# A gated-delta stage with paired transpositions, folded scales and another place for the norm sums

## Chip, cores, metric

One core of one Trainium2 chip runs the whole layer as one program. The metric is the device time of the program in microseconds; the median of three runs of the kernel before is 2038.25 (2031.85 to 2038.56).

## The reference, cut to what matters

One layer of a streaming encoder in float32: a norm, one input projection, chunk-band attention beside a gated delta branch, gates, an output projection and an MLP. The change lies in the gated delta branch (4 heads, key and value width 128, chunks of 64 tokens: 16 chunks of the prompt, and 128 sample tokens that this kernel treats as 2 more chunks). Per chunk and head:

```
k, q    L2-normalised over the 128 channels
gc      = cumsum(g);  decay[i,j] = exp(gc_i - gc_j) for i >= j
a_mat   = strict_lower(beta_i * (k_i . k_j) * decay[i,j]) + I
u, w    = solve(a_mat, [v * beta, k * beta * exp(gc)])
qk      = (q . k^T) * decay;  q_dec = q * exp(gc);  k_dec = k * exp(gc_last - gc)
v_new   = u - w @ s;  o = q_dec @ s + qk @ v_new
s       = s * exp(gc_last) + k_dec^T @ v_new       (chunk after chunk)
out     = rms_norm(o) * gain * silu(z)
```

## The kernel before, in words

The program runs in stages: norm, input projection, attention, delta, tail. The first two and the tail are long runs of products. `stage_delta` (from L1069) takes about 220 us of the span of 2028.7 us.

**Tiling.** 18 chunks of 64 tokens, in groups of four: groups 0 to 3 have four chunks, group 4 has two. Chunks 0 and 1 hold the sample streams, chunks 2 to 17 the prompt. The four heads are laid out as p = 0, 1 and x = 0, 1; x picks the lower or upper 64 partitions, so that one [128, 2, 64] tile holds a quantity of all four heads. Each float32 product appears as two records of the trace, a transposition as one. Chunk n of a group has its own PSUM bank B[n % 4] for its whole preparation.

**Preparation of a chunk**, in steps that go through the engines in turn:

- pair (PE L1702, DVE L1550, POOL L1361): PE multiplies k with q and k, DVE multiplies the result by the decay into KQ, POOL masks the part k.k^T into the levels M[0], M[1] of the block inverse.
- turn (PE L1709, ACT L1449, DVE L1562 and L1563, POOL L1378): PE brings k and v of the four heads from channels-by-tokens to tokens-by-channels, eight products with the identity; ACT writes U0 = v times the key's norm, DVE writes kbe = k exp(gc) and kd = k exp(gc_last - gc); POOL writes S0, a diagonal that holds the row scale s = beta / (norm squared of k).
- x0 (PE L1715, DVE L1570): PE multiplies M[0] by S0, DVE subtracts the result, scaled by s, from S0: the first inverse D, of blocks of two tokens, with the row scale carried in it.
- x0t (PE L1720, ACT L1454, POOL L1365 and L1371): D transposed; POOL makes the remaining levels of M and qk.
- levels 1 to 5, each in a half a (PE L1731, ACT L1466) and a half b (PE L1739, DVE L1582), double the block size of the inverse.
- solve, once for two chunks (PE L1749 and L1752, ACT L1464): w and u into WU.

**Scan.** Chunk after chunk: read (PE L1764 and L1768, ACT L1474, DVE L1592, POOL L1385), write (PE L1775, DVE L1596), out (PE L1780, DVE L1601, ACT L1486). The chunks of group g - 1 are scanned between the preparation steps of group g. For the sample chunks there are "heads" items instead: mask (POOL L1393, L1397), read, out, spread (DVE L1621) and write (PE L1811, DVE L1628), with POOL L1403 for the decay of the states.

**Once for a group.** decay (POOL L1344, PE L1676, ACT L1428); sums (POOL squares q and k in L1335, ACT does it for group 0 in L1433; PE L1682 sums over the channels; DVE L1534 copies the rows); cols (PE L1688 turns the rows into columns, ACT L1438 takes the square root, DVE L1538 to L1542 compute the reciprocal, s and -s); and for the group before, mean (DVE L1636, ACT L1496), norm (DVE L1640, L1641) and two turns (PE L1821, DVE L1649).

**Order.** `schedule()` writes one list by hand, with `between(g)` giving what follows each step of group g; every engine walks the list in its order and skips what it has no part in. So each engine's program order is fixed, and a wait holds up all that stands behind it on that engine. For group g and g + 1 the list reads: pair of the four chunks, then cols(g), then a scan read; turn of four chunks, a scan write; x0 of four, scan out and the next scan read; x0t of four, scan write; and so on; norm(g - 1) behind 4b, its turns behind 5a and 5b; solve, and behind it sums(g + 1).

**Loads.** SP loads the q, k, v channels of a group by `conv(g)` (L1283), one DMA of 12 x 128 rows with 256 tokens, 1 KB for each row (128 tokens, 512 B, for group 4), into C[g % 2]. conv(g) for g >= 2 is issued when the last scan read of group g - 2 is done (L1300), in the first half of group g - 1. Group 0 is loaded in the attention stage in two DMAs (L721 to L723), followed there by the loads of the attention's caches.

```
1116          if g == 1:
...
1118          if g:
1119              out["pair"].insert(0, ("grp", g, "cols"))
...
1124          if g + 1 < NG:
1125              out["2b"].append(("grp", g + 1, "decay"))
1126              out["solve"].append(("grp", g + 1, "sums"))
```

Of the kernel before, what the change touches and what calls it, by code (L numbers as in the profile page):

```python
# [570 lines left out]
def stage_attention(env):  # L571
# [22 lines left out]
    with ExitStack() as c:  # L594
# [90 lines left out]
        def _(sp):  # L685
# [42 lines left out]
            sp.wait_ge(env.c_in, 32)  # L728
# [340 lines left out]
def stage_delta(env):  # L1069
# [35 lines left out]
    def between(g):  # L1105
# [38 lines left out]
    def has(eng, item):  # L1144
# [3 lines left out]
        if kind == "prep":  # L1148
            return {"pair": ("pe", "dve", "pool"), "turn": ("pe", "act", "dve", "pool"), "x0": ("pe", "dve"),
# [46 lines left out]
    with ExitStack() as c:  # L1196
# [6 lines left out]
        C = [env.c0, at("c1", [P, CC, 4 * L], env.c_at + 4 * CC * 4 * L)]  # L1203
        top = env.c_at + 2 * 4 * CC * 4 * L
        o = [at(f"o{i}", [P, 4, 2, P], top + i * 4096) for i in range(2)]
        sq = [at(f"sq{i}", [P, HB, 4 * L], a) for i, a in enumerate((top + 2 * 4096, env.level_at))]
# [9 lines left out]
        S0 = [sb(f"s0{i}", [P, 2, L]) for i in range(4)]  # L1216
# [14 lines left out]
        eg, er, kn2, r2, s_, negs, nk, bq, ms, rso = (vec[:, i, :, :] for i in range(10))  # L1231
# [36 lines left out]

        def kind_of(n):
# [54 lines left out]
        def _(pool):  # L1324
            for item in SCHED:
# [3 lines left out]
                if kind == "grp" and s == "sums":  # L1329
                    w = L * len(GROUPS[n])  # L1330
                    pool.wait_ge(c_in[n % 2], 16 * ((n + 1) // 2))
                    wait(pool, "pe", "grp", n - 1, "sums")
                    for i in range(2):
                        half_c = C[n % 2][:, 4 * i:4 * i + 4, 0:w]
                        pool.tensor_tensor(sq[i][:, :, 0:w], half_c, half_c, ALU.mult).then_inc(sq_made, 1)  # L1335
# [1282 lines left out]
```

## Time and profile before

| what | value |
|---|---|
| median of three runs (lowest, highest) | 2038.25 us (2031.85, 2038.56) |
| the profiled execution: span | 2028.7 us |
| the profiled execution's own time | not listed; the page gives its span alone |
| mean granted clock of TensorE | 0.988 |
| PE busy over the span | 1945.0 us (96%) |
| delta stage, from its first product to the tail's first | 786 to about 1005 us |
| PE busy from 786 to 1006 us | 191.95 us |
| DVE, ACT, POOL busy from 786 to 1006 us | 119.63, 89.17, 96.47 us |

The span runs from the first to the last instruction; the lowest of the three runs is 3.15 us above it, the median 9.55 us. "x8" behind a row counts records: eight records of a product are the four heads of one chunk. Busy time of PE is the union of overlapping products, so a group's mean duration times its count is more than its busy time. What a row costs its engine is best read from the start of one row to the start of the next.

### The profile page before, as it was taken

Reading aid. Unit: us, or ns where it says so; the run is one execution under the profiler, and the core shown is the slowest. Engines: PE = TensorE matmul, PEld = TensorE weight load, DVE = VectorE, ACT = ScalarE, POOL = GpSimd, SP = SyncE. Lnnn points to the kernel's source line nnn. Section 1 sums busy time; section 2 is a strip of 40 time slices with the busy share of each in tenths; the row PEclk is TensorE's granted clock in tenths of the full one; section 3 lists DMA queues with packets and bytes.
Section 4 is the critical chain, followed back from the end, with each engine's and each line's share of the span. In section 5 each row is a group of like instructions: output and inputs, shape, how many; then the busy total and the mean of one; then the engine's idle time right before and its main releaser. Section 6 shows DMA issues by size and latency. Waiting matters only on the chain. (4 is left out here: it accounts for less than half of the span.)

```text
span 2028.7 us, 34282 instructions
## 1 busy us (share of the span) xinstructions
PE 1945.0 (96%) x14050; PEld 1759.9 (87%) x14050; DVE 746.8 (37%) x1482; ACT 634.4 (31%) x1283; POOL 590.6 (29%) x456
## 2 busy tenths in 40 slices
PE   7999999999998888899799999999999999999998
PEld 7899999999994566678699879999999999999997
DVE  5211777111125664565553182222222222222225
ACT  5101222100016664344443245222222222222222
POOL 3111111111132002543354144333333333333333
PEclk9999999999998998999899999999999999999999
DMA  4322223522227213131253232111111111111114
GB/s 119 108 89 88 76 88 118 209 88 88 88 97 238 92 64 84 44 96 39 62 158 105 104 125 88 47 43 42 42 42 42 42 42 42 42 42 42 42 60 169
DMA packets 159273, 169.22 MB, mean 83 GB/s; under 512 B 14187, under 2 KB 130043, under 8 KB 159150
## 3 DMA queue, kind: packets, MB, share of 16 engines
q1 hardware_dynamic: 152814, 141.52, 22.7%
q10 hardware_dynamic: 6336, 25.96, 3.2%
q8 instruction: 89, 1.46, 0.3%
q14 instruction: 34, 0.28, 0.0%
HBM read 126.84 MB, written 40.55 MB: 83 GB/s over the span
## 5 line engine op out<-in xcount | busy, mean ns | idle before, releaser
L2369 DVE TENSOR_TENSOR t_acc<-t_acc,t_B 128x512 f32<-128x512 f32 x252 | 173.3, 688 | 538.6 <-PE t_B L2475 538.6
L116 PE MATMUL i_ps<-x_hi,i_w_lo 128*128 128x384 f32 x1008 | 337.5, 335 | 0.0
L116 PE MATMUL i_ps<-x_hi,i_w_hi 128*128 128x384 f32 x1008 | 337.2, 335 | 0.0
L116 PE MATMUL i_ps<-x_lo,i_w_hi 128*128 128x384 f32 x1008 | 337.2, 335 | 0.0
L2462 PE MATMUL t_B<-t_merged_hi,t_wm_lo 128*128 128x384 f32 x768 | 256.9, 335 | 1.0 <-POOL t_wm_lo L2052 1.0
L2462 PE MATMUL t_B<-t_merged_lo,t_wm_hi 128*128 128x384 f32 x768 | 256.6, 334 | 0.0
L2462 PE MATMUL t_B<-t_merged_hi,t_wm_hi 128*128 128x384 f32 x768 | 256.6, 334 | 0.0
L106 POOL TENSOR_TENSOR i_w_lo<-i_w_raw,i_w_hi 128x1024 fp32r<-128x1024 f32 x44 | 105.4, 2395 | 433.4 <-ACT i_w_hi L101 433.4
L2052 POOL TENSOR_TENSOR t_wm_lo<-t_raw,t_wm_hi 128x1024 fp32r<-128x1024 f32 x49 | 118.8, 2425 | 295.9 <-ACT t_wm_hi L2127 295.9
L116 PEld LDWEIGHTS i_ps<-x_lo,i_w_hi 128*128 128x128 f32 x1008 | 189.8, 188 | 0.0
L116 PEld LDWEIGHTS i_ps<-x_hi,i_w_lo 128*128 128x128 f32 x1008 | 189.7, 188 | 0.0
L116 PEld LDWEIGHTS i_ps<-x_hi,i_w_hi 128*128 128x128 f32 x1008 | 189.6, 188 | 0.0
L2086 POOL TENSOR_TENSOR t_f_lo<-t_f,t_f_hi 128x384 fp32r<-128x384 f32 x96 | 97.5, 1016 | 212.6 <-ACT t_f_hi L2230 212.6
L101 ACT ACTIVATE i_w_hi<-i_w_raw 128x1024 fp32r<-128x1024 f32 x44 | 46.7, 1061 | 349.5 <-PE i_ps L116 324.4
L2127 ACT ACTIVATE t_wm_hi<-t_raw 128x1024 fp32r<-128x1024 f32 x49 | 51.4, 1051 | 316.6 <-PE t_B L2475 314.6
L482 DVE COPY i_out<-i_ps 128x384 f32<-128x384 f32 x78 | 43.5, 558 | 278.6 <-PE i_ps L116 278.6
L2462 PEld LDWEIGHTS t_B<-t_merged_hi,t_wm_lo 128*128 128x128 f32 x768 | 144.2, 188 | 1.8 <-POOL t_wm_lo L2052 1.3
L2462 PEld LDWEIGHTS t_B<-t_merged_lo,t_wm_hi 128*128 128x128 f32 x768 | 144.2, 188 | 0.6
L2462 PEld LDWEIGHTS t_B<-t_merged_hi,t_wm_hi 128*128 128x128 f32 x768 | 144.2, 188 | 0.0
L2475 PE MATMUL t_B<-t_wm_hi,t_f_lo 128*128 128x512 f32 x306 | 121.2, 396 | 0.0
L2475 PE MATMUL t_B<-t_wm_hi,t_f_hi 128*128 128x512 f32 x306 | 120.1, 393 | 0.0
L2475 PE MATMUL t_B<-t_wm_lo,t_f_hi 128*128 128x512 f32 x306 | 120.0, 392 | 0.0
(344 smaller groups left out, 3465.9 us busy)
## 6 DMA issues: line engine op xcount, KB each, us to landing
proj<-i_out ACTq DMA_DIRECT2D x44, 576.0 KB, 2.8
i_w_raw<-in_w_in SPq DMA_DIRECT2D x44, 512.0 KB, 3.9
t_raw<-in_w_up SPq DMA_DIRECT2D x32, 512.0 KB, 4.2
t_raw<-in_w_down SPq DMA_DIRECT2D x32, 512.0 KB, 3.6
t_gates<-proj SPq DMA_DIRECT2D x48, 192.0 KB, 2.7
a_k_cache<-in_cache_attn_k SPq DMA_DIRECT2D x8, 1024.0 KB, 6.1
a_v_cache<-in_cache_attn_v SPq DMA_DIRECT2D x8, 1024.0 KB, 5.3
d_c<-proj SPq DMA_DIRECT2D x3, 1536.0 KB, 7.6
```

What stands on the lines that cost most here:

```text
L101: act.activation(w.hi[s][:, :, :], w.raw[s][:, :, :], ACT.Copy).then_inc(w.hi_made, 1)
L106: pool.tensor_tensor(w.lo[s][:, :, :], w.raw[s][:, :, :], w.hi[s][:, :, :].bitcast(F32), ALU.subtract).then_inc(w.lo_made, 1)
L116: last = pe.matmul(out, a[s][:, c, :], b[:, c, tokens], start=k == 0, stop=k == n - 1)
L482: dve.tensor_copy(st[s][:, g * TG:(g + 1) * TG], ps[3 * s + g][:, 0:TG]).then_inc(free, 1)
L2052: pool.tensor_tensor(flat(lo), flat(raw[n % 2]), flat(h).bitcast(F32), ALU.subtract).then_inc(lo_made, 1)
L2086: pool.tensor_tensor(f_lo[j % 2][a][:, group(g)], f[e % 2][:, :], f_hi[j % 2][a][:, group(g)].bitcast(F32), ALU.subtract).then_inc(f_lo_ma ...
L2127: act.activation(flat(made_in(key)[0]), flat(raw[n % 2]), ACT.Copy).then_inc(hi_made, 1)
L2369: dve.tensor_tensor(a, a, B[(ND * j + d) % 4][:, :], ALU.add).then_inc(added, 1)
L2462: last = pe.matmul(B[5 + e % 3][:, 0:TG], p_[:, cc, :], q_[:, cc, group(g)], start=n == 0, stop=n == 3 * DC - 1)
L2475: done = pe.matmul(B[(ND * min(i, NP_ - 2) + d) % 4][:, :], p_[:, tile(t)], q_[:, cols], start=first and n == 0, stop=last and n == 5)
```

## The change

Six edits in the delta stage, and the layout of its input that follows from them.

1. **Layout.** C holds [slot, channel block, token] in place of [channel block, slot and token]. conv(g) becomes one DMA for each chunk (four for a group, 64 tokens, 256 B for each row), and the load of group 0 in the attention stage becomes four DMAs in place of two. The squares and the sums read the new layout; POOL's copy of q into Qm (L1397) becomes 16 copies of 32 elements for each partition in place of 4 of 128.
2. **turn.** Two heads lie side by side in the new layout, so one full transposition of 128 x 128 turns both: four for a chunk in place of eight products with the identity.
3. **Scale.** The row scale s is multiplied in with the decay: the pair step of DVE becomes two SCALAR_TENSOR_TENSOR of 128 x 128 (decay times s) in place of one TENSOR_TENSOR of 128 x 256; kd takes exp(gc_last - gc) times s (a new column, ers, in the place of -s).
4. **x0.** No product: DVE writes I - M[0] in one TENSOR_TENSOR of 128 x 128. PE's L1715 and POOL's L1378 (S0) go.
5. **x0t** uses the other half of DD and of the bank, since D and its transpose change places.
6. **Order.** sums(g + 1) and cols(g + 1) move from behind solve and behind pair to behind 4b and 5a of group g, ahead of norm and of the first turn (behind 3a and 3b in group 0).

```diff
-            for a, ts in ((0, TP), (P, 0)):
-                sp.dma_start(env.c0[:, :, a:a + P], env.proj[3 * AW:3 * AW + CONV, ts:ts + P].rearrange(
+            for a, ts in enumerate((TP, TP + 64, 0, 64)):
+                sp.dma_start(env.c0[:, a, :, :], env.proj[3 * AW:3 * AW + CONV, ts:ts + 64].rearrange(
                     "(c p) t -> p c t", p=P)).then_inc(env.c_in, 16)
...
-            out["pair"].insert(0, ("grp", g, "cols"))
...
-            out["solve"].append(("grp", g + 1, "sums"))
+            for s, what in zip(("4b", "5a") if g else ("3a", "3b"), ("sums", "cols")):
+                out[s].insert(0, ("grp", g + 1, what))
...
-                ts = first_token(GROUPS[g][0])
-                w = L * len(GROUPS[g])
-                sp.dma_start(C[g % 2][:, :, 0:w], env.proj[3 * AW:3 * AW + CONV, ts:ts + w].rearrange(
-                    "(c p) t -> p c t", p=P)).then_inc(c_in[g % 2], 16)
+                for n in GROUPS[g]:
+                    ts = first_token(n)
+                    sp.dma_start(C[g % 2][:, slot(n), :, :], env.proj[3 * AW:3 * AW + CONV, ts:ts + L].rearrange(
+                        "(c p) t -> p c t", p=P)).then_inc(c_in[g % 2], 16)
...
-                elif s == "turn":
-                    k = slot(n)
-                    wait(pool, "dve", "grp", n // 4, "cols")
-                    if n >= 4:
-                        wait(pool, "dve", "prep", n - 4, "x0")
-                    ins = pool.tensor_tensor(S0[k][:, :, :], bc(env.identc[:, :], 1, 2), bc(s_[:, n, :], 2, L), ALU.mult)
...
-                        src = C[0][:, 0:HB, L * cc:L * cc + L].rearrange("p h (f r t) -> p h f r t", f=2, r=2)
-                        for r in range(2):
-                            ins = pool.tensor_copy(Qm[:, :, cc, r, :, TS * r:TS * r + TS], src[:, :, :, r, :])
+                        for h in range(HB):
+                            src = head_c(cc, h).rearrange("p (f r t) -> p f r t", f=2, r=2)
+                            for r in range(2):
+                                ins = pool.tensor_copy(Qm[:, h, cc, r, :, TS * r:TS * r + TS], src[:, :, r, :])
...
-                        ins = act.activation(DD[k][:, 1, :, :].rearrange("p q m -> p (q m)"), B[k][:, P:2 * P], ACT.Copy)
+                        ins = act.activation(DD[k][:, 0, :, :].rearrange("p q m -> p (q m)"), B[k][:, 0:P], ACT.Copy)
...
-                        ins = dve.tensor_scalar(negs[:, tiles, :], s_[:, tiles, :], -1.0, None, ALU.mult)
+                        if n == 0:
+                            dve.wait_ge(gexp, 3)
+                        ins = dve.tensor_tensor(ers[:, tiles, :], er[:, tiles, :], s_[:, tiles, :], ALU.mult)
...
-                        ins = dve.tensor_tensor(KQ[k][:, :, :, :], B[k][:, 0:256].rearrange("p (q a m) -> p q a m", q=2, a=2),
-                                                bc(E[n // 4 % 2][:, k, :, :], 2, 2), ALU.mult)
+                        wait(dve, "dve", "grp", n // 4, "cols")
+                        for p in range(2):
+                            ins = dve.scalar_tensor_tensor(
+                                out=KQ[k][:, p, :, :], in0=B[k][:, P * p:P * p + P].rearrange("p (a m) -> p a m", a=2),
+                                scalar=s_[:, n, p:p + 1], in1=bc(E[n // 4 % 2][:, k, p, :], 1, 2), op0=ALU.mult, op1=ALU.mult)
...
-                        wait(dve, "dve", "grp", n // 4, "cols")
-                        wait(dve, "pool", "prep", n, "turn")
+                        wait(dve, "pool", "prep", n, "pair")
                         if n >= 4:
-                            wait(dve, "pe", "prep", n - 4, f"{last_level(n - 4)}a")
-                        for p in range(2):
-                            ins = dve.scalar_tensor_tensor(out=DD[k][:, 0, p, :], in0=B[k][:, p * L:p * L + L],
-                                                           scalar=negs[:, n, p:p + 1], in1=S0[k][:, p, :],
-                                                           op0=ALU.mult, op1=ALU.add)
+                            wait(dve, "pe", "prep", solved(n - 4), "solve")
+                        ins = dve.tensor_tensor(DD[k][:, 1, :, :], bc(env.identc[:, :], 1, 2), M[k][:, 0, :, :], ALU.subtract)
...
                         for i in range(2):
-                            for x, p in XP:
+                            for p in range(2):
                                 a = (2 * i + p) * P
-                                ins = pe.matmul(b[half(x), a:a + P], Cn[:, 4 + 4 * i + 2 * p + x, tok(n)], env.ident[:, :],
-                                                start=True, stop=True)
-                    elif s == "x0":
-                        wait(pe, "dve", "prep", n, "turn")
-                        wait(pe, "pool", "prep", n, "turn")
-                        for x, p in XP:
-                            ins = pe.matmul(b[half(x), p * L:p * L + L], M[k][half(x), 0, p, :], S0[k][half(x), p, :],
-                                            start=True, stop=True)
+                                ins = pe.transpose(b[:, a:a + P], Cn[:, k, 4 + 4 * i + 2 * p:6 + 4 * i + 2 * p, :].rearrange("p x t -> p (x t)"),
+                                                   env.ident[:, :])
```

## Rows read from the trace of the kernel before

**Rows 1.** By stretch: length; PE, PEld, DVE, ACT, POOL busy; clock; DMA share; GB/s.

```profile
880.00:910.00 30.00, 28.09 (x642) 24.43 (x640) 18.19 (x54) 16.50 (x58) 17.21 (x23) 1.00 0.18 56
```

**Rows 2.** Timeline of PE, front of group 2: start, length, what, idle before.

```profile
877.24 1.07 PE L1682 MATMUL d_B<-d_sq,pick 128*32 128x256 f32 x16
878.24 1.97 PE L1702 MATMUL d_B<-d_c 128*64 128x128 f32 x32
880.04 0.58 PE L1688 MATMUL d_B<-sel,d_rows 128*64 128x4 f32 x16
...
881.38 3.66 PE L1709 MATMUL d_B<-ident,d_c 128*64 128x128 f32 x64
...
885.62 1.44 PE L1715 MATMUL d_B<-d_s,d_m 64*64 64x64 f32 x32
...
889.14 0.66 PE L1768 MATMUL d_B<-d_state,d_c 128*64 128x128 f32 x8 [1.05 <-DVE d_o L1601]
889.73 1.15 PE L1720 MATMUL d_B<-ident,d_dd 64*64 64x64 f32 x32
```

**Rows 3.** Timeline of PE, later in group 2, behind step 4b.

```profile
910.60 1.14 PE L1731 MATMUL d_B<-d_dd,d_m 64*64 64x64 f32 x32
913.11 0.63 PE L1821 MATMUL d_B<-ident,d_o 128*128 128x128 f32 x4 [1.37 <-DVE d_o L1641]
913.67 1.15 PE L1739 MATMUL d_B<-d_dd,d_x 64*64 64x64 f32 x32
```

**Rows 4.** Timeline of DVE, groups 1 and 2.

```profile
844.40 0.42 DVE L1562 TENSOR_TENSOR d_kbe<-d_B,d_vec 128x256 f32<-128x256 f32 x1
...
847.19 1.27 DVE L1628 TENSOR_TENSOR d_states<-d_states,d_B 128x512 f32<-128x512 f32 x2
...
878.95 1.73 DVE L1550 TENSOR_TENSOR d_kq<-d_B,d_decay 128x256 f32<-128x256 f32 x4
...
886.48 0.74 DVE L1596 TENSOR_TENSOR d_state<-d_state_decayed,d_B 128x256 f32<-128x256 f32 x2
887.14 1.62 DVE L1570 SCALAR_TENSOR_TENSOR d_dd<-d_B,d_vec,d_s 128x64 f32<-128x64 f32 x8
...
911.38 1.58 DVE L1641 TENSOR_TENSOR d_o<-d_o,d_vec 128x1024 f32<-128x1024 f32 x1
913.78 0.88 DVE L1649 SCALAR_TENSOR_TENSOR oa_ob<-d_B,dgain,d_z 128x256 f32<-128x256 f32 x2 [0.81 <-PE d_B L1821]
914.57 0.87 DVE L1582 TENSOR_TENSOR d_dd<-d_dd,d_B 128x128 f32<-128x128 f32 x4
```

**Rows 5.** Timeline of ACT, the second half of solve in group 1.

```profile
877.36 1.09 ACT L1464 ACTIVATE d_wu<-d_B 128x512 f32<-128x512 f32 x2 [1.27 <-PE d_B L1752]
```

**Rows 6.** Timeline of POOL: the copies of q, the squares of groups 2 and 3.

```profile
818.83 1.01 POOL L1397 COPY d_q_masked<-d_c 128x128 f32<-128x128 f32 x4
...
861.96 3.75 POOL L1335 TENSOR_TENSOR d_sq<-d_c 128x1024 f32<-128x1024 f32 x2 [7.49 <-DMA d_c<-proj]
...
908.14 3.75 POOL L1335 TENSOR_TENSOR d_sq<-d_c 128x1024 f32<-128x1024 f32 x2 [8.34 <-DMA d_c<-proj]
```

**Rows 7.** Timeline of SP's queue: the loads of groups 2 and 3.

```profile
854.33 0.37 SPq L1285 DMA_DIRECT2D d_c<-proj  x1
...
899.66 0.37 SPq L1285 DMA_DIRECT2D d_c<-proj  x1
```

**Rows 8.** Busy time by stretch, around the loads of groups 3 and 4.

```profile
900.00:908.00 8.00, 7.84 (x202) 6.68 (x196) 4.66 (x13) 5.56 (x14) 0.00 (x0) 1.00 0.63 201
942.00:948.00 6.00, 6.00 (x154) 5.31 (x152) 3.52 (x9) 3.98 (x14) 0.69 (x2) 1.00 0.49 134
```

**Rows 9.** Busy time by stretch, near the end of the stage.

```profile
993.00:997.00 4.00, 3.48 (x32) 2.52 (x30) 1.59 (x4) 1.30 (x6) 2.73 (x2) 0.57 0.00 0
```

**Rows 10.** Timeline of PE around the sample states' last products.

```profile
834.13 2.08 PE L1811 MATMUL d_B<-d_w_masked,d_kd 64*128 64x512 f32 x4 [2.76 <-DVE d_w_masked L1621]
836.14 1.93 PE L1682 MATMUL d_B<-d_sq,pick 128*32 128x256 f32 x16
```

More of the change, by code:

```diff
@@ L727, in _ @@
             sp.wait_ge(saved, 16 * 6)
-            sp.wait_ge(env.c_in, 32)
+            sp.wait_ge(env.c_in, 64)
         @block.gpsimd
@@ L1148, in has @@
         if kind == "prep":
-            return {"pair": ("pe", "dve", "pool"), "turn": ("pe", "act", "dve", "pool"), "x0": ("pe", "dve"),
+            return {"pair": ("pe", "dve", "pool"), "turn": ("pe", "act", "dve"), "x0": ("dve",),
                     "x0t": ("pe", "act", "pool"), "solve": ("pe", "act")}.get(
@@ L1201, in at @@
             return nc.alloc_sbuf_tensor_at("d_" + name, shape, F32, offset=offset)
-        C = [env.c0, at("c1", [P, CC, 4 * L], env.c_at + 4 * CC * 4 * L)]
+        C = [env.c0, at("c1", [P, 4, CC, L], env.c_at + 4 * CC * 4 * L)]
         top = env.c_at + 2 * 4 * CC * 4 * L
         o = [at(f"o{i}", [P, 4, 2, P], top + i * 4096) for i in range(2)]
-        sq = [at(f"sq{i}", [P, HB, 4 * L], a) for i, a in enumerate((top + 2 * 4096, env.level_at))]
+        sq = [at(f"sq{i}", [P, 4, HB, L], a) for i, a in enumerate((top + 2 * 4096, env.level_at))]
         t1 = at("t1", [P, 2, 2, P], top + 3 * 4096)
@@ L1230, in stage_delta @@
         vec = sb("vec", [P, 10, NC, 2])
-        eg, er, kn2, r2, s_, negs, nk, bq, ms, rso = (vec[:, i, :, :] for i in range(10))
+        eg, er, kn2, r2, s_, ers, nk, bq, ms, rso = (vec[:, i, :, :] for i in range(10))
         gm = sb("gm", [P, 96])
@@ L1267, in U_of, with head_c, landed @@
             return pairs(WU[n % 8][:, 256:512])
+        def head_c(n, c):
+            return chunk_c(n)[:, slot(n), c, :]
+        def landed(g):
+            return 16 * sum(len(GROUPS[i]) for i in range(2 - g % 2, g + 1, 2))
         def kind_of(n):
@@ L1329, in _ @@
                 if kind == "grp" and s == "sums":
-                    w = L * len(GROUPS[n])
-                    pool.wait_ge(c_in[n % 2], 16 * ((n + 1) // 2))
+                    m = len(GROUPS[n])
+                    pool.wait_ge(c_in[n % 2], landed(n))
                     wait(pool, "pe", "grp", n - 1, "sums")
                     for i in range(2):
-                        half_c = C[n % 2][:, 4 * i:4 * i + 4, 0:w]
-                        pool.tensor_tensor(sq[i][:, :, 0:w], half_c, half_c, ALU.mult).then_inc(sq_made, 1)
+                        half_c = C[n % 2][:, 0:m, 4 * i:4 * i + 4, :].rearrange("p m h t -> p m (h t)")
+                        pool.tensor_tensor(sq[i][:, 0:m, :, :].rearrange("p m h t -> p m (h t)"), half_c, half_c,
+                                           ALU.mult).then_inc(sq_made, 1)
                     continue
@@ L1388, in _ @@
                     pool.wait_ge(cleared, 4)
-                    pool.wait_ge(env.c_in, 32)
+                    pool.wait_ge(env.c_in, 64)
                     for x in range(2):
@@ L1430, in _ @@
                     elif s == "sums":
-                        act.wait_ge(env.c_in, 32)
+                        act.wait_ge(env.c_in, 64)
                         for i in range(2):
-                            act.activation(sq[i][:, :, 0:w], C[0][:, 4 * i:4 * i + 4, 0:w], ACT.Square).then_inc(sq_made, 1)
+                            act.activation(sq[i][:, :, :, :].rearrange("p m h t -> p m (h t)"),
+                                           C[0][:, :, 4 * i:4 * i + 4, :].rearrange("p m h t -> p m (h t)"), ACT.Square
+                                           ).then_inc(sq_made, 1)
                         continue
@@ L1681, in _ @@
                             for h in range(HB):
-                                last = pe.matmul(Z7[32 * h:32 * h + 32, 0:w], env.pick[:, 31 - i:63 - i], sq[i][:, h, 0:w],
+                                last = pe.matmul(Z7[32 * h:32 * h + 32, 0:w], env.pick[:, 31 - i:63 - i], sq[i][:, 0:len(mine), h, :],
                                                  start=i == 0, stop=i == 1)
@@ L1694, in _ @@
                         if n == 0:
-                            pe.wait_ge(env.c_in, 32)
+                            pe.wait_ge(env.c_in, 64)
                         elif n % 4 == 0:
-                            pe.wait_ge(c_in[n // 4 % 2], 16 * ((n // 4 + 1) // 2))
+                            pe.wait_ge(c_in[n // 4 % 2], landed(n // 4))
                         if n >= 4:
@@ L1701, in _ @@
                             h = 2 * p + x
-                            ins = pe.matmul(b[half(x), 2 * L * p:2 * L * p + 2 * L], Cn[:, 4 + h, tok(n)], Cn[:, h:h + 5:4, tok(n)],
+                            ins = pe.matmul(b[half(x), 2 * L * p:2 * L * p + 2 * L], head_c(n, 4 + h), Cn[:, k, h:h + 5:4, :],
                                             start=True, stop=True)
@@ L1719, in _ @@
                         for x, p in XP:
-                            ins = pe.matmul(b[half(x), P + p * L:P + p * L + L], DD[k][half(x), 0, p, :],
+                            ins = pe.matmul(b[half(x), p * L:p * L + L], DD[k][half(x), 1, p, :],
                                             env.ident[half(x), half(x)], start=True, stop=True)
@@ L1767, in _ @@
                         for x, p in XP:
-                            ins = pe.matmul(Z1[half(x), p * P:p * P + P], chunk_c(n)[:, 2 * p + x, tok(n)], S[:, x, p, :],
+                            ins = pe.matmul(Z1[half(x), p * P:p * P + P], head_c(n, 2 * p + x), S[:, x, p, :],
                                             start=True, stop=True)
```

10 lines of the change are left out of this document (4 added, 6 removed).

## The prediction

> **What bounds the kernel now.** I read the stretches first. In a steady stretch of the delta stage PE is busy 28.09 of 30 us, while DVE has 18.19, ACT 16.50 and POOL 17.21 [rows 1]. PE sets the pace, and a product taken off it should be worth its time, as long as no other engine is late. So the second view is the timeline of PE at the front of a group [rows 2]: the turn takes 3.66 us for four chunks, and behind it PE idles 1.05 us for an output sum of DVE. The cover is thin there. Third, DVE's timeline [rows 4], since DVE follows PE through this front. Fourth, POOL's squares: POOL idled 8.34 us for the load of group 3 before 908.14 [rows 6]. The load was early enough only because sums came last in the group; 4b ends at 910.60 [rows 3]. All times are of the profiled execution (span 2028.7); I carry the difference over to the median of 2038.25, which lies 9.55 above that span. The three runs spread over 6.7 us, and a difference under 0.5% (10.2 us) is about what a measurement of this kernel can't tell from none.
>
> **The ceiling.** A set of four transpositions starts 0.56 us before what follows (913.11 to 913.67, [rows 3]). Four chunks take 2.24 instead of 3.66: 1.42 saved. x0 goes whole: 885.62 to the next start, some 1.28 [rows 2]. That is 2.7 for four chunks, 12.1 for 18. If PE stayed the bound everywhere, 12 us would be the gain.
>
> **The front of a group, walked.** Zero is 877.24, where solve's products end [rows 2]; before, sums takes 1.00, cols some 0.45, and x0t starts at 12.49.
> - Pair: 0.45 a chunk (878.24 to 880.04 for four, [rows 2]). Chunks 0 and 1 at 0 to 0.9. Chunk 2 needs the bank that ACT empties until 878.45, that is 1.21 [rows 5]: the moved sums covered this. Pair ends at 2.17, after 0.35 idle.
> - DVE's pair becomes two instructions. An SCALAR_TENSOR_TENSOR of 64 columns costs 0.20 (1.62 for 8), of 256 columns 0.40 (0.79 for two), so 128 columns by interpolation 0.27 (bounds 0.20 and 0.40): 0.53 a chunk against 0.43 [rows 4]. Four end at 3.15, ahead of the last turn; at 0.80 a chunk they end near 4.3, still ahead.
> - The scan read ends at 3.05, turn at 5.3. DVE cannot start kbe before ACT has chunk 0, near 4.55, and back to back needs 0.34 for each of eight (844.40 to 847.19 holds all eight, 2.79, [rows 4]): to 7.25. Then the state sums, 0.66, to 7.9; x0 as four 128-column TENSOR_TENSOR at 0.2, as in 914.57 [rows 4], to 8.7; the output sum 0.35, to 9.05.
> - PE: scan write and out to 6.45, idle to 8.0 for the state, half a read, idle to 9.1 for the output sum, the other half, and x0t at 9.7.
>
> So x0t is 2.8 earlier, of which 1.45 only moved. 1.35 is real, half the ceiling: the removed products leave PE waiting for kbe, kd and the state on DVE. In group 4 (two chunks) the same walk gives 1.75, of which 0.8 moved. POOL loses S0 (four instructions), which lay beside other work: nothing. ers replaces -s one for one: nothing.
>
> **The moved sums, and the loads.** conv(3) is issued at 899.66 [rows 7], its squares start at 908.14 [rows 6]: 8.48 us. It has 1536 packets of 1 KB, and afterwards 6144 of 256 B. No row shows such packets. From [rows 8]: 0.63 of 8 us on 16 engines is 52.5 ns for 1 KB; 0.49 of 6 us for the same 1536 packets of 512 B in group 4 is 30.6 ns. Lower bound: bytes alone count, nothing added (a gain is excluded, since no packet gets larger). Upper bound: 256 B costs as much as 512 B, 11.75 us busy for 5.04, so 6.7 added. I take the line through both, 19.7 ns, hence 7.56 busy, 2.5 added; it is nearest to the 512 B row. Landing takes 11.0. SP issues three more DMAs, 0.4 each, inside that time.
> The Trainium skill (DMA: Bandwidth & Descriptors, Specifications) wants 512 B for line rate, with read-modify-write below. By that rule the sum would go by the upper bound or past it.
>
> Group 2: shifted by the front, conv(3) goes at 19.6 on the scale above, lands at 30.6, is squared by 34.35 (3.75, [rows 6]). PE is through 4b at 30.6 and now waits there, since sums stands ahead of 5a; behind it queue 5a, cols, the first turn of group 1's output and 5b. Sums end near 34.9, DVE copies the rows until 35.6, and norm, which now stands behind that copy on DVE, needs 1.8 more (reciprocal and 1.58, [rows 4]): the first turn starts at 37.3 instead of 35.87 (913.11). **Group 2 ends 1.4 later.** With the lower bound it would end 1.1 earlier, with the upper one 5.6 later.
> Group 1: conv(2) is issued at 854.33 [rows 7] and squared from 861.96 [rows 6], 7.63 later; with 2.5 more and 3.75 of squares it is through at 868.2, where that group's 4b ends by the count of its steps: it just fits. But norm behind the row copy starts the first turn 1.15 later.
> Group 3: the load has half the bytes and fits; norm's delay costs 0.45 there.
>
> **Groups 0 and 1, front.** In group 0 x0t is 1.7 earlier by the same walk, sums and cols, now before the first solve, take 1.45 of it back. POOL's 16 small copies for 4 [rows 6]: 0.25 each before for 128 elements; an estimate of 0.14 for 32, between 0.06 (by elements) and 0.25 (by count). 2.2 for 1.0, on the chain ACT, POOL, PE, POOL, DVE to 834.13 [rows 10]: +1.2 (bounds 0 and +3). Net, group 1 starts 0.95 later, but sums (836.14, 1.93 at the low clock) is gone there. DVE, full with the sample states, is then the bound: x0t 0.85 earlier, after PE has idled 2.7. That is as long as the 2.76 ahead of 834.13, behind which products took twice their time [rows 10]: level 1.2 GHz. I count one fall: from 993 to 997 PE was busy 3.48 us at a mean clock of 0.57 [rows 9]; some 3.2 us at half speed, 1.6 lost.
>
> **Sum**, against the span: group 1, -0.85 + 1.6 + 1.15 = +1.9; group 2, +1.4; group 3, -2.8 + 0.45 = -2.35; group 4, -1.75. Together -0.8, say -1: **2037**. The load of group 0 in the attention stage gets two more DMAs on SP ahead of the caches; I cost it at nothing, since those are loaded a batch ahead, and at 3 us of issue if that cover fails.
>
> **Rivals.**
> 1. *PE stays the bound* (chance 0.14): DVE or ACT turn out quicker in the front, the load arrives within 9 us, no clock falls. For it: PE's 94% in [rows 1]. Against: the 1.05 of idle already there [rows 2]. Full ceiling -12, so 2026; with half of the lost part back, -7: 2031.
> 2. *The small packets decide* (0.13), the one that ends slower. The place is the squares of groups 2 and 3, which PE now meets ahead of 5a. If 256 B costs as much as 1 KB, 52.5 ns, a full group's load takes 15.1 longer: groups 1 and 2 some 12.5 each above the sum, group 3 some 4: +28, so 2066. Each 10 ns above 19.7 costs 3.8 in each of two groups; it passes 10.2 slower from about 33 ns. Against it: the 512 B packets moved nearly as fast as their bytes would.
> 3. *The clock falls in every front* (0.20). The fronts of groups 2 to 4 get 2.5 of idle in 6 us, as much as before the slow stretch at 834 [rows 10]. Each fall costs 1.6: +5, so 2042; with the load's upper bound 2048. Against: at 889 idle of 1.05 left the clock at 1.00 [rows 1, 2].
> A page would make more of it: the Trainium skill (TensorE: Matmul & The Clock Gate, Part 4) says that transposition mode does not count as TensorE work for the clock. By that, each front would be idle from 3.05 to 8; if a fall then lasts twice as long, four fronts cost 3.2 each: 2050. No row here has transpositions alone long enough to show it; this is a part, 0.05, of the 0.20.
> 4. *Near nothing, by the sum* (0.53): 2033 to 2043. That the change does not do what it says I hold excluded by the diff.
>
> **Range and chances.** 2028 to 2048 leaves out the best end of rival 1, all past the upper bound of the load, and the clock with both. Faster by over 0.5% needs almost the whole ceiling: 0.08. Slower: rival 2 and the worst of 3: 0.17. Same: 0.75.
>
> **What would show it.** Right: a turn of some 2.2 for four chunks, PE idle near 2 us ahead of the second scan read, waiting for DVE's state; x0t some 9.7 behind solve; POOL's squares of group 3 starting near 11 us behind the issue, and PE idle ahead of sums in group 2 but not in 1 and 3. Wrong: a landing above 15 us or below 9, a granted clock of 0.5 in groups 2 to 4, or a DVE pair above 0.8.

## The result, and the profile after

The changed kernel takes 2055.18 us (median of 4 runs, 2049.82 to 2058.15) against 2035.14 for the kernel before, run beside it (4 runs): ratio 1.0101, 95% interval 1.0076 to 1.0126. A second set of four runs gave 2054.09, ratio 1.0115 (1.0088 to 1.0142). The forecast was 2037 in 2028 to 2048, one less than 2038.25. It was wrong: the change costs some 20 us.

The page's first part, of the changed kernel:

```profile
span 2056.4 us, 33533 instructions
PE 1952.4 (95%) x13690; PEld 1762.6 (86%) x13690; DVE 756.2 (37%) x1482; ACT 634.8 (31%) x1283; POOL 584.2 (28%) x450
```

Busy times say little here; the stage's length says more. Busy time by stretch, the whole delta stage (length, busy of PE, PEld, DVE, ACT and POOL with instructions in brackets, clock, DMA share, GB/s), first before:

```profile
786.29:1005.02 218.73, 190.97 (x3811) 159.23 (x3811) 118.36 (x320) 88.19 (x298) 96.18 (x116) 0.94 0.22 63
```

and after, with three short stretches that are used below:

```profile
794.44:1034.12 239.68, 192.88 (x3450) 159.05 (x3450) 124.57 (x320) 87.68 (x298) 91.24 (x110) 0.87 0.25 58
890.00:902.00 12.00, 12.00 (x101) 10.21 (x103) 2.71 (x9) 2.17 (x4) 1.78 (x3) 0.50 0.15 45
954.00:958.00 4.00, 1.04 (x16) 0.58 (x12) 4.00 (x10) 0.05 (x1) 1.93 (x2) 0.84 0.00 0
958.00:962.00 4.00, 2.63 (x38) 2.30 (x40) 1.74 (x4) 1.87 (x8) 4.00 (x6) 0.50 0.02 4
```

The stage is 20.95 longer. PE has 361 records fewer and yet is busy 1.9 us longer, at a mean granted clock of 0.87 for 0.94; its idle time (length less busy) went from 27.8 to 46.8. The five groups, from the start of one pair step to the next, were 44.2, 40.2, 42.9, 40.7 and 43.2; they are 48.4, 47.7, 49.9, 44.2 and 41.9. The loss is in groups 0 to 3. (The attention stage in front was 7.7 longer in this profile, 198.4 for 190.7; it does not come from the change, as the experiments show.)

PE's timeline after (start, length, what, idle before), the moved sums for group 3 and then that group's front, which answers to [rows 2]:

```profile
935.67 0.64 PE L1685 MATMUL d_B<-d_sq,pick 128*32 128x256 f32 x8 [0.96 <-POOL d_sq L1340]
...
937.43 0.64 PE L1685 MATMUL d_B<-d_sq,pick 128*32 128x256 f32 x8 [1.12 <-POOL d_sq L1340]
...
948.03 1.09 PE L1705 MATMUL d_B<-d_c 128*64 128x128 f32 x16
949.29 1.09 PE L1705 MATMUL d_B<-d_c 128*64 128x128 f32 x16 [0.16 <-ACT d_wu L1467]
...
951.19 1.97 PE L1712 MATMUL d_B<-ident,d_c 128*128 128x128 f32 x16
953.08 0.71 PE L1772 MATMUL d_B<-d_v_new,d_kd 64*128 64x128 f32 x8
956.14 0.66 PE L1761 MATMUL d_B<-d_state,d_wu 128*64 128x128 f32 x8 [1.76 <-DVE d_state L1599]
959.37 1.12 PE L1765 MATMUL d_B<-d_state,d_c 128*64 128x128 f32 x8 [2.58 <-DVE d_o L1604]
960.42 1.97 PE L1717 MATMUL d_B<-ident,d_dd 64*64 64x64 f32 x32
```

The turn of four chunks starts 1.89 before what follows (3.66 before [rows 2]). The state is read 8.11 behind the pair's start. The other half of that read waits another 2.58, for an output sum of DVE, and comes at half clock (1.12 for eight records, where the eight of the first half took 0.66). DVE's timeline in the same front:

```profile
948.74 2.38 DVE L1558 SCALAR_TENSOR_TENSOR d_kq<-d_B,d_vec,d_decay 128x128 f32<-128x128 f32 x8 [4.50 <-PE d_B L1705]
951.30 0.42 DVE L1595 TENSOR_TENSOR d_v_new<-d_wu,d_B 128x256 f32<-128x256 f32 x1 [0.18 <-PE d_B L1765]
...
954.92 0.41 DVE L1570 TENSOR_TENSOR d_kd<-d_B,d_vec 128x256 f32<-128x256 f32 x1
955.25 0.74 DVE L1599 TENSOR_TENSOR d_state<-d_state_decayed,d_B 128x256 f32<-128x256 f32 x2
955.91 3.07 DVE L1575 TENSOR_TENSOR d_dd<-identc,d_m 128x128 f32<-128x128 f32 x4
958.91 0.41 DVE L1604 TENSOR_TENSOR d_o<-d_t,d_B 128x256 f32<-128x256 f32 x1
```

and POOL's, with its copies of q and its squares for group 3:

```profile
830.39 2.45 POOL L1398 COPY d_q_masked<-d_c 128x32 f32<-128x32 f32 x16
...
933.63 3.74 POOL L1340 TENSOR_TENSOR d_sq<-d_c 128x1024 f32<-128x1024 f32 x2 [9.89 <-DMA d_c<-proj]
...
956.07 1.04 POOL L1385 TENSOR_TENSOR d_state_decayed<-d_state,d_g_last 128x512 f32<-128x512 f32 x1 [2.86 <-DVE d_state L1599]
957.07 1.31 POOL L1371 TENSOR_TENSOR d_m<-d_kq,levc 128x512 f32<-128x512 f32 x1
958.34 0.50 POOL L1377 TENSOR_TENSOR d_qk<-d_kq,cumc 128x128 f32<-128x128 f32 x1
```

The four subtractions I - M[0] take 3.07, where the sum had 0.8. They begin 0.16 ahead of POOL's decay of the state, and the fourth ends at 958.98, 0.14 behind the end of POOL's third instruction (958.34 + 0.50). They look held, one by one, by whatever POOL is running. Taken singly in the trace, 15 of the stage's 18 subtractions began while POOL was running an instruction, and each ended 0.15 us behind that instruction's end; the three that began with POOL idle took 0.28. The source view of line 1575 (count, then ns least/median/most, first and last start):

```profile
L1575 DVE TENSOR_TENSOR d_dd<-identc,d_m x18: 280/554/1348, 810.1 to 997.7; 128x128 f32<-128x128 f32 x18
```

It is 280 ns when free, and up to 1348 when not. Line L1595 at 951.30 is a TENSOR_TENSOR too, with one operand in PSUM, and it took its usual 0.42 although POOL was masking at the time (L1367, from 949.43 to 952.22 in the trace). By groups of instructions in the stage (busy us, mean ns of one | idle before):

```profile
L1575 DVE TENSOR_TENSOR d_dd<-identc,d_m 128x128 f32<-128x128 f32 x18 | 13.2, 791 | 0.0
...
L1558 DVE SCALAR_TENSOR_TENSOR d_kq<-d_B,d_vec,d_decay 128x128 f32<-128x128 f32 x36 | 10.4, 345 | 19.2 <-PE d_B L1705 18.9
```

18 of them have 13.2 us instead of 18 x 0.2 = 3.6. The theory, called A in the expectations: a TENSOR_TENSOR of DVE whose two inputs both lie in SBUF waits for the POOL instruction that is running; its wait delays the output sum and x0t, PE idles, and the clock falls. Rivals: the moved sums (theory B), the layout with its small packets and copies (theory C), and the transpositions.

### The profile page after: what moved, and what is told of

It reads as the page before. It is cut to its first block and busy times, and to the rows that moved or that the text cites. A ratio compares the mean times of both kernels' runs of the same rounds, so it can differ in the third digit from the quotient of the medians.

```text
span 2056.4 us, 33533 instructions
## 1 busy us (share of the span) xinstructions
PE 1952.4 (95%) x13690; PEld 1762.6 (86%) x13690; DVE 756.2 (37%) x1482; ACT 634.8 (31%) x1283; POOL 584.2 (28%) x450
```

## The experiments

"Stage" is the delta stage's length in the one profiled execution (218.7 before, 239.7 after), so a few us of it can be that execution's own. Each ratio is one of medians, against runs of the kernel before that were made beside it.

**I - M[0] on POOL.** The changed kernel; only the engine of x0 is another, with the waits that go with it.

```diff
-                        ins = dve.tensor_tensor(DD[k][:, 1, :, :], bc(env.identc[:, :], 1, 2), M[k][:, 0, :, :], ALU.subtract)
+                    ins = pool.tensor_tensor(DD[k][:, 1, :, :], bc(env.identc[:, :], 1, 2), M[k][:, 0, :, :], ALU.subtract)
```

> The changed kernel, with I - M[0] made by POOL (one TENSOR_TENSOR a chunk, in the step x0) in place of DVE. In the changed kernel DVE's four x0 instructions of group 3 took 3.07 us where 0.8 was forecast, while POOL ran its own products; the state read behind them came late and the granted clock fell. Theory A (DVE and POOL hold each other up where both work on SBUF alone, and the low clock follows from that idle time): x0t of group 3 begins about 10 us behind solve's end instead of 12.4, the clock stays at 1.00 in groups 2 and 3, the stage from its first product to the tail's first goes from 239.7 to 226 to 231 us, the time to 2041 to 2047. Theory B (the moved sums and cols are the cost): the stage stays within 3 us of 239.7. Theory C (the loads in small packets): as B.

Measured 2037.37 (10 runs), ratio 1.0008 (0.9985 to 1.0030); stage 222.38:

```profile
795.70:1018.08 222.38, 185.49 (x3450) 152.30 (x3451) 110.36 (x302) 87.26 (x298) 97.97 (x128) 0.91 0.27 62
```

17.3 us of the 21 go with one instruction's engine. DVE has 14.2 less, POOL 6.7 more. Stage and time are better than the forecast's 226 to 231 and 2041 to 2047; the clock did not stay at 1.00 in groups 2 and 3, but fell for some 3 us in each.

**The new layout alone.** The kernel before, with loads by chunk, squares by chunk and 16 small copies.

```diff
-                sp.dma_start(C[g % 2][:, :, 0:w], ...
+                for n in GROUPS[g]:
+                    sp.dma_start(C[g % 2][:, slot(n), :, :], ...
```

> The kernel before, with the new layout alone: one load a chunk in rows of 256 B, squares and sums on it, POOL's 16 small copies; the eight products of turn, x0 and the order as before. Theory C (small packets): the attention stage is 6 to 8 us longer and the delta stage 5 or more, the time 2045 or more. Theory A: the delta stage gains 1 to 3 us over 218.7, since the squares of group 3 are not waited for at the end of the group; the attention stage is longer by 0 to 8 us, which theory A does not settle: 8 if it came from the two more loads ahead of the caches, 0 if the low clock there came by chance. Theory B: no change in the delta stage.

Measured 2033.80, ratio 1.0005 (0.9983 to 1.0027); stage 222.25, of which 3.0 in group 0. Groups 1 to 4 are within 0.6 us of before: 256-byte packets cost at most that there. The gain of 1 to 3 us that theory A gave did not come.

**Sums and columns moved, alone.** The kernel before, with the two steps in mid-group.

```diff
-            out["pair"].insert(0, ("grp", g, "cols"))
-            out["solve"].append(("grp", g + 1, "sums"))
+            for s, what in zip(("4b", "5a") if g else ("3a", "3b"), ("sums", "cols")):
+                out[s].insert(0, ("grp", g + 1, what))
```

> The kernel before, with sums and cols moved into the group (behind 4b and 5a) and nothing else. Theory B (the moved sums are the cost): the delta stage is 8 us or more longer than 218.7. Theory A: 0 to 3 us longer, from norm behind the row copy and from the bank that ACT empties; the time 2033 to 2040. Theory C: no change, the packets are as before.

Measured 2037.23, ratio 1.0019 (0.9999 to 1.0038); stage 219.14, with group 2 1.7 longer, as the sum had it (1.4). This kernel has the new order but not the new layout, and its attention stage took 198.5; the one with the layout alone has 191.3, and the repeated changed kernel 190.2. The changed kernel itself thus took 198.4 in one profile and 190.2 in another: those 7.7 us come and go from run to run.

**Layout and transpositions.** The kernel of the layout, with the turn by transposition.

```diff
-                            for x, p in XP:
-                                ins = pe.matmul(b[half(x), a:a + P], head_c(n, 4 + 4 * i + 2 * p + x), env.ident[:, :],
+                            for p in range(2):
+                                ins = pe.transpose(b[:, a:a + P], Cn[:, k, 4 + 4 * i + 2 * p:6 + 4 * i + 2 * p, :]...
```

> The kernel before, with the new layout and the four transpositions a chunk; x0 stays a product whose DVE part reads PSUM, the order is as before. Theory A: the delta stage is 2 to 4 us shorter than with the layout alone, at most 6 (1.42 a group of four by the rows), and DVE's x0 is not stretched. If transpositions let the clock fall by themselves, the granted clock drops to 0.5 behind the turns of groups 2 to 4 and the stage is 5 us or more longer than with the layout alone. Theory B: as A. Theory C: no difference to the layout alone.

Measured 2031.14, ratio 0.9994 (0.9972 to 1.0015); stage 219.89. The fronts of groups 2 and 3 are 10.55 from pair to x0t for 11.48: 0.9 of the turn's 1.4 is real. The stage's mean clock is 0.93 for 0.94, so transpositions did not bring it down.

**I - M[0] with one operand in PSUM.** The changed kernel; DVE still makes it, as two instructions that read 0 times a bank, less M[0]. The identity is left out, so the time alone counts.

```diff
-                        ins = dve.tensor_tensor(DD[k][:, 1, :, :], bc(env.identc[:, :], 1, 2), M[k][:, 0, :, :], ALU.subtract)
+                        for p in range(2):
+                            ins = dve.scalar_tensor_tensor(out=DD[k][:, 1, p, :], in0=B[k][:, p * L:p * L + L],
+                                                           scalar=0.0, in1=M[k][:, 0, p, :], op0=ALU.mult, op1=ALU.subtract)
```

> The changed kernel, with x0 still on DVE, in the same place and behind the same waits, but as two SCALAR_TENSOR_TENSOR of 64 columns that read PSUM (zero times the bank, minus M[0]). It leaves out the identity in I - M[0], so what is computed downstream is another number; the work is the same. This is more work on DVE than the change's one TENSOR_TENSOR (0.4 us a chunk against 0.2 when nothing is in the way). Theory A (an instruction of DVE with both operands in SBUF waits while POOL works on SBUF): the four chunks take 1.6 to 1.8 us instead of 3.07, x0t of group 3 begins 10 to 11 us behind the first pair instead of 12.39, the stage is 228 to 234 us instead of 239.7. If what made x0 slow was a wait for M[0] or for the bank, it stays as slow, and the stage stays above 238.

Measured 2042.43 (10 runs, 2031.92 to 2054.60), ratio 1.0044 (1.0020 to 1.0068); the profiled execution's stage is 222.15. DVE's timeline in the front of group 3, then POOL's:

```profile
933.07 0.74 DVE L1601 TENSOR_TENSOR d_state<-d_state_decayed,d_B 128x256 f32<-128x256 f32 x2
933.72 1.14 DVE L1576 SCALAR_TENSOR_TENSOR d_dd<-d_B,d_m 128x64 f32<-128x64 f32 x8
934.77 0.41 DVE L1606 TENSOR_TENSOR d_o<-d_t,d_B 128x256 f32<-128x256 f32 x1
```

```profile
933.88 1.04 POOL L1385 TENSOR_TENSOR d_state_decayed<-d_state,d_g_last 128x512 f32<-128x512 f32 x1 [2.85 <-DVE d_state L1601]
```

Eight instructions take 1.14 beside the same decay of POOL, where four took 3.07. The engine, the place in the order and the neighbour are the same, and the operation was ruled out above (L1595): where the operands lie makes the difference. The time is not wholly back, though. The profiled run was the quickest of ten, so its stage, shorter than the 228 to 234 forecast, says little of the version; by the medians (ratio 1.0044 for 1.0101 and 1.0115) it gives back some 12 to 14 us and stays 9 above the kernel before.

**The x0 product back as filler.** The changed kernel, with the removed product computed twice on PE into a bank that nobody reads, to test the clock's part.

```diff
+                        for r in range(2):
+                            for x, p in XP:
+                                ins = pe.matmul(b[half(x), p * L:p * L + L], M[k][half(x), 0, p, :], env.identc[half(x), :], ...
```

> The changed kernel with filler on PE: in the place of the removed x0 product, each chunk gets it twice, on M[0] and a constant, into the part of the bank that x0t writes next; nothing reads it. It lies in the idle time ahead of the second scan read, and DVE's slow x0 stays. If the low clock behind that idle time is a cost of its own, it stays at 1.00 in the fronts of groups 2 and 3, and the stage is 3 to 7 us shorter than 239.7, although PE does more. If the clock costs nothing beyond the wait, the stage is the same or 1 to 4 us longer.

Measured 2046.39, ratio 1.0058 (1.0038 to 1.0078); stage 236.09. The clock did not stay at 1.00: it was 0.50 from 896.0 to 899.4 and from 950.6 to 954.0, in the fronts of groups 2 and 3, half as long as without the filler. Group 1 fell from 47.7 to 43.0, but group 2 rose to 52.9 with the clock at 0.50 from 927 to 940. Against the changed kernel, some 9 to 12 us come back by the ratios though PE has more to do. That fits a price of the low clock, but since the filler didn't control where the clock falls, it does not show it.

**Sums late.** The changed kernel, with sums and columns behind solve again.

```diff
-            for s, what in zip(("4b", "5a") if g else ("3a", "3b"), ("sums", "cols")):
-                out[s].insert(0, ("grp", g + 1, what))
+            out["solve"] += [("grp", g + 1, "sums"), ("grp", g + 1, "cols")]
```

> The changed kernel with sums and cols of the next group behind solve, ahead of the next pair (cols cannot stand behind pair as before, since pair now needs s). Theory B (the moved sums are the cost) expects the stage at 225 us or less. Theory A: PE waits at each group's start for the chain sums, rows, cols, square root, reciprocal, some 2 to 4 us a group, and gives up the wait for norm, 1 to 2 a group; DVE's slow x0 stays: 238 to 248.

Measured 2050.74 (4 runs), ratio 1.0065 (1.0040 to 1.0091); stage 235.61. The stage is 4.1 us shorter, and less than the 238 to 248 of theory A, but far from the 225 of theory B. By the ratios 7 to 10 us come back (the intervals 1.0040 to 1.0091 and 1.0076 to 1.0126 just overlap), though the same move cost the kernel before only 0.4 us of stage. So the order is not the cause by itself, but some of the loss may come only where it and the slow x0 stand together.

**A try to do better.** x0 on POOL, 4 copies of q for 16, and sums and columns behind the output turns in 5a and 5b.

```diff
+            for s, what in zip(("5a", "5b") if g else ("3a", "3b"), ("sums", "cols")):
+                out[s].insert(len(out[s]) if g else 0, ("grp", g + 1, what))
```

> Meant to beat both kernels: the changed kernel with I - M[0] on POOL (as in the first of these runs), sums and cols behind the two output turns (behind 5a and 5b) instead of ahead of norm and of the first turn, and POOL's copies of q again four of 128 elements. Against the run with I - M[0] on POOL alone (stage 222.4): groups 1 to 3 lose the wait of norm behind the row copy (0.5 to 1.5 each) and group 2 the wait for its load, group 0 the 1.5 of the small copies: stage 214 to 219, the time 2028 to 2034 where the kernel before has 2034.

Measured 2047.21, ratio 1.0061 (1.0037 to 1.0085); stage 235.90 at a mean clock of 0.86. A miss: the front was shorter (10.4 to x0t in group 2), but groups 1 to 3 took 47.2, 49.3 and 46.6. Moved there, sums and columns and the output turns wait for one another over a shared bank; I read that from the order of steps and did not test it by itself.

**The suspect alone, in the kernel before.** One subtraction I - M[0] a chunk is added on DVE, into a tile that its own instruction then overwrites. Of the change it has only the wait that goes with it (DVE stood idle for it nowhere in the front below).

```diff
                         if n >= 4:
-                            wait(dve, "pe", "prep", n - 4, f"{last_level(n - 4)}a")
+                            wait(dve, "pe", "prep", solved(n - 4), "solve")
+                        dve.tensor_tensor(DD[k][:, 1, :, :], bc(env.identc[:, :], 1, 2), M[k][:, 0, :, :], ALU.subtract)
```

> The kernel before with the suspected instruction alone added: in x0, ahead of DVE's own two, the TENSOR_TENSOR of 128 x 128 in SBUF (constant minus M[0]) once a chunk, its result overwritten later. Nothing else changes, and it costs 0.2 us when nothing is in the way, 0.8 a group, 3.6 in all. Theory A: it waits for POOL's products as in the changed kernel, 2 to 3 us in each of groups 1 to 3, and some of it brings the low clock: the stage is 6 to 14 us longer than 218.7. Without such a hold-up it is 0 to 3 us longer.

Measured 2052.20 (4 runs), ratio 1.0088 (1.0062 to 1.0114). The stage:

```profile
786.50:1026.23 239.73, 198.19 (x3810) 165.42 (x3810) 132.18 (x337) 89.31 (x298) 96.69 (x116) 0.91 0.20 58
```

The 18 added subtractions (the stage's count of DVE instructions rises by 17; the source view of L1569, the added line, lists all 18) make it 21.0 longer, as long as the whole change makes it, and beyond the 6 to 14 that was forecast. DVE's timeline, then POOL's beside it:

```profile
946.81 0.28 DVE L1569 TENSOR_TENSOR d_dd<-identc,d_m 128x128 f32<-128x128 f32 x1
947.01 0.47 DVE L1571 SCALAR_TENSOR_TENSOR d_dd<-d_B,d_vec,d_s 128x64 f32<-128x64 f32 x2
947.40 0.76 DVE L1569 TENSOR_TENSOR d_dd<-identc,d_m 128x128 f32<-128x128 f32 x1
948.08 0.46 DVE L1571 SCALAR_TENSOR_TENSOR d_dd<-d_B,d_vec,d_s 128x64 f32<-128x64 f32 x2
948.47 0.96 DVE L1569 TENSOR_TENSOR d_dd<-identc,d_m 128x128 f32<-128x128 f32 x1
949.35 0.46 DVE L1571 SCALAR_TENSOR_TENSOR d_dd<-d_B,d_vec,d_s 128x64 f32<-128x64 f32 x2
949.73 1.37 DVE L1569 TENSOR_TENSOR d_dd<-identc,d_m 128x128 f32<-128x128 f32 x1
```

```profile
946.97 1.04 POOL L1385 TENSOR_TENSOR d_state_decayed<-d_state,d_g_last 128x512 f32<-128x512 f32 x1 [2.62 <-DVE d_state L1597]
947.97 1.31 POOL L1365 TENSOR_TENSOR d_m<-d_kq,levc 128x512 f32<-128x512 f32 x1
949.24 0.49 POOL L1371 TENSOR_TENSOR d_qk<-d_kq,cumc 128x128 f32<-128x128 f32 x1
949.70 1.26 POOL L1365 TENSOR_TENSOR d_m<-d_kq,levc 128x512 f32<-128x512 f32 x1
```

Here each wait can be read singly. The first added subtraction starts before POOL does: 0.28. The others end at 948.16, 949.43 and 951.10; POOL's instructions end at 948.01, 949.28 and 950.96. Each ends 0.14 to 0.15 behind the end of the one POOL instruction that was running as it began. The SCALAR_TENSOR_TENSOR between them read PSUM and keep their 0.46 for two beside the same POOL work.

**The changed kernel again.**

> The changed kernel again. The attention stage took 198.4 us in it and 190.7 in the kernel before; the kernel with only sums and cols moved took 198.5 there, the one with only the layout changed 191.3. If the 7.7 us are a chance state of the clock, it takes about 191 or about 198.5, whichever comes; if they belong to the loads, 198 again. The delta stage stays at 236 to 242, the ratio at 1.006 to 1.012.

Measured 2054.09, ratio 1.0115 (1.0088 to 1.0142); stage 239.20, its groups within 0.6 of the first profile's; the attention stage 190.2.

**x0 on POOL, 4 copies for 16.** The first experiment's kernel, with q of a chunk copied in two instructions as before.

```diff
-                        for h in range(HB):
-                            src = head_c(cc, h).rearrange("p (f r t) -> p f r t", f=2, r=2)
+                        src = C[0][:, cc, 0:HB, :].rearrange("p h (f r t) -> p h f r t", f=2, r=2)
```

> The changed kernel with I - M[0] on POOL and POOL's copies of q again as four of 128 elements. The copies take 1.0 instead of 2.45 us on the chain of group 0: the stage is 1 to 3 us shorter than the 222.4 with 16 copies, the time 2031 to 2036.

Measured 2036.40 (10 runs), ratio 1.0008 (0.9992 to 1.0024), the same time as with 16 copies within the noise. The stage, then POOL's four subtractions:

```profile
785.90:1004.73 218.83, 181.14 (x3451) 148.99 (x3451) 109.36 (x301) 87.31 (x298) 96.49 (x116) 0.94 0.27 63
```

```profile
928.41 1.71 POOL L1373 TENSOR_TENSOR d_dd<-identc,d_m 128x128 f32<-128x128 f32 x4
```

At the clock of before, 0.94, PE is busy 9.8 less and idle 9.9 more (27.8 to 37.7): what the removed products free is waited away. In the trace PE's longest waits there are 5.2 us for the state (DVE L1598), 3.7 for the squares at the moved sums (POOL L1340) and 2.6 for the columns (DVE L1552). The kernel before has none of these three, but waits 6.6 for the norm (DVE L1641), which is 3.8 here (L1643).

**Layout, transpositions, 4 copies.** The kernel before with these alone; its edits stand above.

> Meant to beat both kernels: the kernel before with the new layout, the four transpositions, and four copies of q; x0 remains a product whose DVE part reads PSUM, sums and cols stay behind solve and pair. Against the same with 16 copies (stage 219.9): 1 to 3 us shorter, 217 to 219 where the kernel before has 218.7; the transpositions' gain of 1 to 1.5 a group of four remains, the ratio to the kernel before 0.997 to 1.000.

Measured 2032.54 (12 runs), ratio 0.9992 (0.9976 to 1.0008); stage 221.58, longer than the 217 to 219 forecast, with the last group at 47.2 and the clock at 0.50 from 991 on to the stage's end. No version that I tried is measurably quicker than the kernel before.

## Why the prediction was wrong

**The step that failed** is in the walk of the front: "x0 as four 128-column TENSOR_TENSOR at 0.2, as in 914.57, to 8.7". The row's instruction has as many columns, but one of its operands is d_B, in PSUM. The new one has both in SBUF, and DVE then waits for the POOL instruction that is running: the four took 3.07 us for the 0.8 in the sum. I had matched the shape and not where the operands lie. Up to there the walk holds. On its scale in group 3, the state sums end at 7.96 (7.9 forecast) and the state is read at 8.11 (8.0); then x0 ends at 10.95 for 8.7, the output sum at 11.3 for 9.05, and x0t starts at 12.39 for 9.7.

The kernel before had given a hint. The norm, a product with both operands in SBUF, took 1.58 at 911.38 [rows 4], while POOL's squares ran until 911.89 [rows 6]. With POOL idle the same line took less:

```profile
868.88 1.22 DVE L1641 TENSOR_TENSOR d_o<-d_o,d_vec 128x1024 f32<-128x1024 f32 x1
```

I put 1.58 into the sum without asking why the other was shorter. The Trainium skill (SBUF — State Buffer, Who interferes with whom) has the rule: a DVE instruction with two SBUF inputs contends with a GpSimd instruction (POOL here) that reads SBUF, and the order of issue decides which of the two blocks. The added subtraction's rows agree, with ends 0.14 to 0.15 behind POOL's. I had not weighed that rule.

**How 2.25 us a front become 21.** Against the same kernel with x0 on POOL, the changed one has 9.9 more of PE's idle time (46.8 for 36.9) and 7.4 more of busy time for the same products (192.88 for 185.49), at 0.87 for 0.91. The first part is near the 9.6 us by which 18 instructions exceed their 3.6. The second is products at half clock: between 954 and 958 PE was busy 1.04 of 4 us, and in the next 4 the clock is 0.50; from 890 to 902 it is 0.50 with PE full. In the kernel before, the clock is 1.00 from 840 to 992. The added subtraction in the kernel before shows the same pair: clock 0.91 for 0.94, 7.2 more busy, 13.8 more idle. How much of the idle time is the wait itself, and how much follows from slower products upstream, isn't separated.

The long stretch at half clock (888.5 to 902.1) is not behind a front. The waits ahead of it are in the middle of group 1, the second of them for the chain of the moved columns:

```profile
880.92 0.45 PE L1736 MATMUL d_B<-d_x,d_dd 64*64 64x64 f32 x8 [1.54 <-ACT d_x L1469]
...
886.97 0.63 PE L1818 MATMUL d_B<-ident,d_o 128*128 128x128 f32 x4 [1.32 <-DVE d_vec L1547]
```

The repeated changed kernel has the same stretch (880.0 to 893.6), again behind waits at the moved sums and columns (1.12 and 1.33). With x0 on POOL the 1.33 stands there too, behind 0.74, and the clock stays at 1.00. Two profiles of each kernel say that this part of the loss goes with the slow x0, but not through the wait at a front. The last kernel above (layout, transpositions, 4 copies) has a long fall too, with neither the slow x0 nor the moved sums. So what brings such a stretch stays open.

By groups, the sum had +1.9 for groups 0 and 1 together, +1.4, -2.35 and -1.75 for the others; they came out at +11.7, +7.0, +3.5 and -1.3.

**The other steps.**
- The ceiling and its half: of the 12 us in products, 9.8 showed in the version with x0 on POOL and 4 copies, and all of it was waited away (2036.40, ratio 1.0008). That is near the forecast's number, for another kernel than the one forecast, and by partly other waits: the state on DVE as walked, but also the moved sums and columns.
- The turn was a little better than 2.24: 1.89. DVE's pair instruction took 0.30 of timeline (2.38 for 8) for 0.27. PE's wait for ACT's bank was 0.16 for 0.35.
- The small packets: the load of group 3 was issued at 923.61 and squared from 933.63, 10.0 later (forecast 11.0, between 8.5 and 15.2). Rival 2 is out: with the layout alone groups 1 to 4 kept their lengths. PE did wait for the squares at the moved sums, as forecast, 0.96 and 1.12 us in PE's timeline above.
- The copies of q: 2.45 for 2.2. Group 0 with the layout alone was 3.0 longer, the upper bound that I gave.
- Sums moved: group 2 1.7 longer by itself, for 1.4.
- The loads ahead of the attention stage: nothing, as forecast. The 7.7 us came in a kernel without them and stayed away in kernels with them.
- Rival 3, a clock fall in each front, came true in groups 2 and 3, with the granted clock of 0.5 there that the forecast had named as a sign of being wrong; but it came behind the slow x0, and idle and price were too small. I gave each front 2.5 of idle and each fall 1.6, where in group 3 the second wait alone is 2.58, behind the 1.76 of the first, and the clock is 0.50 for 6.8 us (956.7 to 963.5). PE is busy 4.22 of these, so some 2.1 are lost there by estimate; the long stretch in group 1 loses some 6.8 (half of 13.6), and it was in no part of the walk. Its part on transpositions is not borne out: with layout and transpositions alone the clock stayed at 0.93 and the fronts got shorter. The Trainium skill (TensorE: Matmul & The Clock Gate, Part 4) says that transposition mode does not count as TensorE work for the clock; no run here has transpositions without products around them, so that stays untested.

**Open:** why the clock falls in one group and not in the next (the filler moved the long fall from group 1 to group 2), how order and slow x0 act together, and why the version with the PSUM operand spreads over 23 us.

## What to carry to other kernels

Price a new DVE instruction by a row that has the same shape and the same places of operands: here, with both in SBUF, it lasted until the POOL instruction beside it was done, up to 1.35 us for 0.28, and what followed it on DVE waited too. Products taken off PE, the bound engine, gained nothing here (2036.40 and 2032.54 for 2034.09), because the engines that feed it came late at the same place, and with longer waits the clock was lower as well. When two rows of one line differ (1.22 and 1.58 here), find out why before using either.

## What the runs showed that I had not expected

- A DVE subtraction of 128x128 float32 with both operands in SBUF took 0.28 us free and up to 1.35 beside POOL. POOL's own masking (128x512) was hardly touched: 1.26 to 1.32 in the changed kernel, 1.26 to 1.29 in the one before.
- 18 such instructions added to the kernel before, some 5 us of work if free (18 x 0.28), lengthened it by 18 us, 2052.20 for 2034.09.
- Half clock came with PE full, for 12 us on end (890 to 902, busy 12.00), behind waits of 1.54 and 1.32 us. Half of that time is lost, by estimate, more than the waits themselves.
- Sixteen transpositions, each of two heads, took 1.89 us from start to next start, where the 32 products (64 records) that did the same took 3.66.
- 256-byte packets: a load of 6144 was in use 10.0 us after its first issue, where the same bytes in 1536 packets of 1 KB took 8.5.
